# A two-block transformer kernel in fp32: two row norms deferred to the evictions behind them

## The chip, the cores and the metric

The program runs on one core of a Trainium2 chip. The metric is the device time of the whole program in microseconds, from a median of three runs. Engines are named as in the profile: PE is TensorE, DVE is VectorE, ACT is ScalarE, POOL is GpSimd, SP is SyncE, which issues the weight loads. "q" behind a name is the engine's queue, PEld a weight load into the PE array.

## The reference

256 tokens, width 2048, fp32 throughout. Two blocks follow one another; what matters for the change is where the norms stand:

```
# block 1
h = x
h = h + mixer_block(rms_norm(h, norm_mix_w), w_in, ...)      # projections, scan, attention, w_out
u = rms_norm(h, norm_mlp_w)                                  # "norm 1" below
h = h + jnp.square(jax.nn.relu(u @ w_up)) @ w_down
h = rms_norm(h, norm_final_w)
# block 2
h = concatenate([meta_tokens, h])                            # 16 tokens ahead
hn = rmsnorm(h, pre_norm_g)                                  # with the line before: "norm 2"
qa, ka, va, ga, qb, kb, vb, gb = split(hn @ w_in_2)
y = concatenate([axial attention(qa, ka, va) * silu(ga), differential attention(qb, kb, vb) * silu(gb)]) @ w_out_2
out = (h + rmsnorm(y, post_norm_g))[16:]
```

A norm multiplies each row (token) by r = 1/sqrt(mean(row^2) + eps) and each column by a weight. Since r is one number for each token, (r * row) @ W = r * (row @ W), and relu(r * z)^2 = r^2 * relu(z)^2.

## The kernel before

Every product is made from fp32 values split in two: hi is the value rounded to the fp32r format, lo the rest, and three products hi*hi, hi*lo, lo*hi are summed. Weights come in chunks of 256 rows by 512 columns (`raw`, 4 slots). For each chunk ACT makes the upper part (`split_hi`, L695), DVE the lower one (`split_lo`, L986), and PE does its matmuls: `chunk_t` (L351), 24 of them, with the result transposed (features on partitions, 256 tokens as columns, 272 with the meta tokens), or `chunk_n` (L363), 12 with 512 columns and rows as rows. Eight chunks make one column group, whose result lies in one of two PSUM sets of two banks each (`set_free` counts evictions). The split of a chunk waits until PE is done with the chunk four before it, so ACT and DVE, which follow the same program order, run one chunk behind PE's end and three ahead of its need.

The order of all work is written out by hand: each engine has its own list, and side work (scan levels, attention steps) is hung between the chunks of a group. In the second block this is `side(pos)`, where pos counts chunks from column group 6 of the second in-projection: unit u of the attention is scored at one position, exponentiated at the next, normalised on DVE two later, turned on PE three later, multiplied with the values four later. 16 units of the differential attention start at position 0, 16 of the axial one at position 28.

The stages in order: first norm, first in-projection (22 groups) with scan and attention, branches, out-projection (4 groups, `chunk_n`, added onto h by DVE at L1190), **norm 1**, MLP in four quarters (4 groups up, `chunk_t`, ACT relu L845, POOL square L1457; 4 groups down, `chunk_n`, added onto h at L1210), **norm 2**, second in-projection (13 groups, j = 0 to 12; the first five are keys and values, evicted by ACT from 272-column banks), last projection (4 groups) and output.

A norm (`norm`, L701 on ACT, L988 on DVE, `turn_normed`, L371, on PE) runs between two groups: ACT squares each group of h and sums the rows (L699), DVE adds the sums, ACT takes the root (L704), DVE the reciprocal, both scale the rows into `normed` (token tile 0 on DVE at L998, tile 1 on ACT at L708), PE transposes 32 tiles (L381) into banks 4 to 7, ACT writes `xhi` with the column weight (L711), DVE `xlo` (L1001), and the next projection starts on them. For norm 2, h is also multiplied by the final norm's weights, squared once more (L1215, L858), and two scales are combined (L1222 to L1231).

In the second in-projection ACT evicts every group (`evac_in2`, L868): groups 0 to 3 (L873, L877), 4 (L879 to L881), queries (L884), queries with their squares for the rope (L888, L889), and for the gates a sigmoid (L738) that DVE multiplies with the same PSUM data (L1261). In group 8, `rope` on POOL (L1466 to L1472) works on `qg`, which the next eviction overwrites.

## Time and profile before

| | |
|---|---|
| median of 3 runs | 2041.23 us (2040.49 to 2042.9) |
| span of the profiled execution | 2039.5 us |
| PE busy | 1968.3 us, 97% |
| DVE busy | 1124.5 us, 55% |
| ACT busy | 900.0 us, 44% |
| POOL busy | 191.6 us, 9% |
| DMA | 345.29 MB, mean 169 GB/s |
| granted PE clock, by 40 slices | 9 tenths or more in all |

The profile is of one execution; its span is what the views below refer to, and it lies 1.0 to 3.4 us below the three times. Times in the timeline are from the span's start. A busy PE row is the duration of one matmul as modelled; the distance between starts is what a matmul costs in a sequence.

### The profile page before, as it was taken

How to read it: one execution, taken by the hardware profiler on the slowest of the kernel's cores; microseconds unless marked ns; L12 is line 12 of the kernel's file. 1: busy time of each engine (PE TensorE's matmuls, PEld its weight loads, DVE VectorE, ACT ScalarE, POOL GpSimd, SP SyncE). 2: the span in 40 equal slices, each digit the busy share in tenths (PEclk: the TensorE clock that was granted, in tenths of full speed). 3: DMA queues.
4: the chain of work that ended last, by engine and by line, in shares of the span. 5: the costliest groups of instructions: out<-in, count | busy, mean ns of one | idle time of the engine just before them, and what ended most of it. 6: DMA issues, size and time to landing. Idle time of an engine off the chain costs nothing.

```text
span 2039.5 us, 34252 instructions
## 1 busy us (share of the span) xinstructions
PE 1968.3 (97%) x13542; PEld 1802.6 (88%) x13542; DVE 1124.5 (55%) x1185; ACT 900.0 (44%) x1165; POOL 191.6 (9%) x110
## 2 busy tenths in 40 slices
PE   5999999999999998999999999999989999998997
PEld 5989999898899987998998899899869998878986
DVE  4456877476545645445444444544455447686554
ACT  5443333356443445443444344344444335535543
POOL 2002433110000100000000000000000000032100
PEclk9999999999999999999999999999999999999999
DMA  7664555555565564666666666666554654333553
GB/s 195 178 190 144 165 162 165 171 175 150 146 207 176 188 213 136 187 189 190 184 187 187 187 187 186 191 180 194 187 186 124 175 157 127 110 106 113 157 189 129
DMA packets 175089, 345.29 MB, mean 169 GB/s; under 512 B 10896, under 2 KB 11024, under 8 KB 174176
## 3 DMA queue, kind: packets, MB, share of 16 engines
q1 hardware_dynamic: 173184, 337.75, 55.7%
q0 software_dynamic: 1776, 5.64, 1.1%
q8 instruction: 103, 1.69, 0.3%
q14 instruction: 26, 0.21, 0.0%
HBM read 341.25 MB, written 2.10 MB: 168 GB/s over the span
## 4 chain that ended last, share of the span: by engine, by line
PE 91%; DVE 5%; ACT 2%; POOL 1%; issue 1%; DMA 1%; DVEq 0%; SPq 0%; ACTq 0%; POOLq 0%
PE ps L351 53%; PE ps L363 31%; DVE wlo L986 1%; PE ps L408 1%; ACT whi L695 1%; DVE obr L1310 1%; PE ps L621 1%; DMA x_nat<-in_x_dram 1%; DVE rs_hg L1100 1%; DVE qsq L1244 0%; DVE xlo L1001 0%; PE ps L591 0%; PE ps L465 0%; PE ps L609 0%; PE ps L455 0%
## 5 line engine op out<-in xcount | busy, mean ns | idle before, releaser
L986 DVE TENSOR_TENSOR wlo<-raw,whi 128x1024 fp32r<-128x1024 f32 x632 | 809.4, 1289 | 788.5 <-ACT whi L695 788.0
L695 ACT ACTIVATE whi<-raw 128x1024 fp32r<-128x1024 f32 x632 | 664.8, 1059 | 993.2 <-PE ps L351 663.7
L351 PE MATMUL ps<-xhi,whi 128*128 128x256 f32 (+1 forms) x3008 | 859.3, 286 | 9.5 <-DVE wlo L986 3.7
L351 PE MATMUL ps<-xlo,whi 128*128 128x256 f32 (+1 forms) x3008 | 847.1, 282 | 0.0
L351 PE MATMUL ps<-xhi,wlo 128*128 128x256 f32 (+1 forms) x3008 | 846.4, 281 | 0.0
L351 PEld LDWEIGHTS ps<-xhi,whi 128*128 128x128 f32 x3008 | 569.1, 189 | 24.6 <-issue 15.7
L351 PEld LDWEIGHTS ps<-xlo,whi 128*128 128x128 f32 x3008 | 568.8, 189 | 1.9 <-issue 1.0
L351 PEld LDWEIGHTS ps<-xhi,wlo 128*128 128x128 f32 x3008 | 568.3, 189 | 0.0
L363 PE MATMUL ps<-whi,xhi 128*128 128x512 f32 x256 | 101.1, 395 | 0.0
L363 PE MATMUL ps<-whi,xlo 128*128 128x512 f32 x256 | 101.1, 395 | 0.0
L363 PE MATMUL ps<-whi,ya_lo 128*128 128x512 f32 x256 | 101.0, 395 | 0.0
L363 PE MATMUL ps<-wlo,yb_hi 128*128 128x512 f32 x256 | 101.0, 395 | 0.0
L363 PE MATMUL ps<-whi,ya_hi 128*128 128x512 f32 x256 | 101.0, 395 | 0.0
L363 PE MATMUL ps<-wlo,ya_hi 128*128 128x512 f32 x256 | 101.0, 395 | 0.0
L363 PE MATMUL ps<-whi,yb_hi 128*128 128x512 f32 x256 | 101.0, 395 | 0.0
L363 PE MATMUL ps<-whi,yb_lo 128*128 128x512 f32 x256 | 101.0, 394 | 0.0
L363 PE MATMUL ps<-wlo,xhi 128*128 128x512 f32 x256 | 100.6, 393 | 0.0
L1457 POOL TENSOR_TENSOR relu<-relu 128x1024 f32<-128x1024 f32 x16 | 32.2, 2013 | 695.8 <-ACT relu L845 695.8
L1396 POOL TENSOR_TENSOR acc<-acc,masked 128x1024 f32<-128x1024 f32 x14 | 40.0, 2858 | 270.6 <-DVE masked L1082 270.6
L363 PEld LDWEIGHTS ps<-wlo,yb_hi 128*128 128x128 f32 x256 | 48.2, 188 | 11.3
L363 PEld LDWEIGHTS ps<-whi,ya_lo 128*128 128x128 f32 x256 | 48.2, 188 | 11.3
L363 PEld LDWEIGHTS ps<-whi,yb_hi 128*128 128x128 f32 x256 | 48.2, 188 | 11.2
...
## 6 DMA issues: line engine op xcount, KB each, us to landing
...
raw<-in_w_up_dram SPq DMA_DIRECT2D x128, 512.0 KB, 3.8
raw<-in_w_down_dram SPq DMA_DIRECT2D x128, 512.0 KB, 4.2
...
```

The lines of the kernel that those rows point to most:

```text
L351: ins = mm(outs[b], w[:, k % SLOTS, j, cols], v[:, kt, 0:n], start=start, stop=last and j == CK - 1 and i == 2, skip_group_check=True)
L363: ins = mm(ps[:, 2 * s + t, :], v[:, kt, toks], w[:, k % SLOTS, j, :], start=first and j == 0 and i == 0, stop=last and j == CK - 1 and i ...
L408: ins = mm(misc[:, i // 4, (i % 4) * P:(i % 4 + 1) * P], kr[:, hd, toks], qp[:, hd, toks], start=True, stop=True)
L621: mm(ps[:, 7, 0:P], v_meta[:, vh, :], pt2[0:META, u % 2, T:T + P], start=False, stop=True).then_inc(u_pv, 1)
L695: f(whi[:, k % SLOTS], raw[:, k % SLOTS], ACT.Copy).then_inc(whi_ready, 1)
L986: tt(wlo[:, k % SLOTS], raw[:, k % SLOTS], whi[:, k % SLOTS], ALU.subtract).then_inc(wlo_ready, 1)
L1100: nc.vector.reciprocal(rs_hg[:, 2 * i:2 * i + 2, :], rs_hg[:, 2 * i:2 * i + 2, :]).then_inc(hg_rs, 1)
L1310: nc.vector.reciprocal(obr[:, 2 * i:2 * i + 2, :], obr[:, 2 * i:2 * i + 2, :]).then_inc(bn_rs, 1)
L1396: tt(acc[:, half, :], acc[:, half, :], masked[:, half, :], ALU.add).then_inc(hg_acc, 1)
L1457: tt(relu2[:], relu[:], relu[:], ALU.mult).then_inc(up_sq, 1)
```

## The change

Norms 1 and 2 no longer stand between two groups. PE transposes the raw rows of h, one column group at a time, eight 128x128 tiles ahead of the third chunk of the next group (`turn_group`); ACT and DVE write the two parts with the column weights alone (`turned_upper`, `turned_lower`), for norm 1 into new buffers `x2hi`, `x2lo`, for norm 2 into `xhi`, `xlo` with the weight `fin_k`, the product of the final norm's and the second block's weights, which one more small load brings. The per-token scale is applied later. For the MLP its square multiplies each down group on eviction (two DVE operations on 128x512 in place of one on 128x1024). For the second in-projection the scale is wanted along the columns, so DVE makes two diagonal matrices, PE multiplies ones by them after group 0, and DVE copies the result to `row_s`; PE waits for that (`r_ready`) ahead of group 1. DVE then evicts all 13 groups with a multiplication by `row_s`. What ACT did at these evictions it does from SBUF (square and scale of the rope queries) or, for the gates, as a sigmoid that reads DVE's copy and writes PSUM, which DVE multiplies as before. The multiplication of h by the final norm's weights moves to POOL. The PE loops of the out-projection and the first MLP quarter are written out.

The diff, cut to its core (`...` marks what is left out):

```diff
+            def turn_group(b, n, freed):
+                pe.wait_ge(set_free[n % 2], freed)
+                if n >= 2:
+                    pe.wait_ge(x_ready, KT * b + 4 * n - 4)
+                for i in range(4):
+                    kt = 4 * n + i
+                    for t in range(NT):
+                        ins = nc.tensor.transpose(turned(n, i)[:, t * P:(t + 1) * P],
+                                                  h[:, t, kt * P:(kt + 1) * P], ident[:])
+                    if i % 2 == 1:
+                        ins.then_inc(n_tr, 1)
...
-            with pe.Fori(0, 2) as i:
-                for s in range(2):
-                    pe.wait_ge(set_free[s], G_IN // 2 + 4 + i)
-                    for k in range(NC):
+            for n in range(4):
+                pe.wait_ge(set_free[n % 2], G_IN // 2 + 4 + n // 2)
+                for k in range(NC):
+                    if n == 0:
                         pe.wait_ge(br_ready, k // 2 + 1)
-                        chunk_n(C_OUT + 2 * NC * i + NC * s, k, CK * k, xhi, xlo, s, k == 0, k == NC - 1)
-            turn_normed(1)
-            def quarter(q):
+                    if n >= 1 and k == 2:
+                        turn_group(1, n - 1, out_free[n - 1])
+                    chunk_n(C_OUT + NC * n, k, CK * k, xhi, xlo, n % 2, k == 0, k == NC - 1)
...
+                        if first and g == 0:
+                            if k == 2:
+                                turn_group(1, 3, out_free[3])
                             pe.wait_ge(x_ready, KT + CK * (k + 1))
-                        chunk_t(c0 + NC * g, k, CK * k, xhi, xlo, blocks(g % 2), T, k == 0, k == NC - 1)
+                        chunk_t(c0 + NC * g, k, CK * k, x2hi, x2lo, blocks(g % 2), T, k == 0, k == NC - 1)
...
+                        if last and g >= 1 and k == 2:
+                            turn_group(2, g - 1, down_free[g - 1])
...
                     if j == 0:
+                        if k == 2:
+                            turn_group(2, 3, down_free[3])
                         pe.wait_ge(x_ready, 2 * KT + CK * (k + 1))
...
+                if j == 0:
+                    pe.wait_ge(r_diag, NT)
+                    for t in range(NT):
+                        ins = mm(ps[:, 4, t * P:(t + 1) * P], ones[:], diag[:, t, :], start=True, stop=True)
+                    ins.then_inc(r_mm, 1)
...
+            def turned_upper(b, n, dst, w):
+                for i in range(4):
+                    kt = 4 * n + i
+                    act.wait_ge(n_tr, KT // 2 * b + kt // 2 + 1)
+                    f(dst[:, kt, 0:T], turned(n, i), ACT.Copy, scale=w[:, kt:kt + 1]).then_inc(n_hi, 1)
...
             for n in range(4):
                 for k in range(NC):
                     split_hi(C_OUT + NC * n, LEAD + k)
-                h_squares(1, n, G_IN // 2 + 4 + n // 2 + 1, n_ss)
-            norm(1, h, mlp_w, 2)
-            def quarter(q, last):
+                    if n >= 1 and k == 0:
+                        h_squares(n - 1, out_free[n - 1], n_ss, junk_out)
+                    if n >= 1 and k == 1:
+                        turned_upper(1, n - 1, x2hi, mlp_w)
...
+                if j == 4:
+                    act.wait_ge(set_free[0], SETS_BEFORE_2 + 3)
+                    f(qsq[:, 0:2, :], qg[:, 0:2, :], ACT.Square).then_inc(nr_ev, 1)
+                    act.wait_ge(nr_ev, 1)
+                    f(qg[:, 0:2, :], qg[:, 0:2, :], ACT.Copy, scale=gvec[:, 2:3]).then_inc(nr_ev, 1)
                 elif j in (7, 8):
                     n = j - 6
-                    act.wait_ge(nr_done, n)
-                    f(qg[:, :, 0:T], pset(n - 1), ACT.Copy, scale=gvec[:, 1:2]).then_inc(nr_ev, 1)
-                    f(qsq[:, :, 0:T], pset(n - 1), ACT.Square).then_inc(nr_ev, 1)
-                else:
-                    g = (j - 9)
+                    act.wait_ge(nr_raw, n)
+                    f(qsq[:, :, 0:T], qg[:, :, 0:T], ACT.Square).then_inc(nr_ev, 1)
+                    act.wait_ge(nr_ev, 2 * n + 1)
+                    f(qg[:, :, 0:T], qg[:, :, 0:T], ACT.Copy, scale=gvec[:, 1:2]).then_inc(nr_ev, 1)
+                elif j >= 9:
+                    g = j - 9
                     dst = gb if g < 2 else ga
-                    sigmoid(dst[:, 4 * (g % 2):4 * (g % 2) + 4, :], g % 2, e_sig)
+                    act.wait_ge(g_raw, g + 1)
+                    f(pset(g % 2), dst[:, 4 * (g % 2):4 * (g % 2) + 4, :], ACT.Sigmoid).then_inc(e_sig, 1)
...
+                    if j == 0:
+                        if k == 0:
+                            h_squares(3, down_free[3], f_sq, junk)
+                        if k == 1:
+                            turned_upper(2, 3, xhi, fin_k)
+                        if k == 2:
+                            scaled_squares(3)
+                        if k == 3:
+                            act.wait_ge(f_un, 1)
+                            f(ss[:, 4:6], ss[:, 4:6], ACT.Sqrt, bias=eps_t[:], scale=1.0 / D).then_inc(f_un, 1)
+                        if k == 4:
+                            row_root(2, 6)
...
+            def turned_lower(b, n, dst, hi, w):
+                for i in range(4):
+                    kt = 4 * n + i
+                    dve.wait_ge(n_hi, KT * b + kt // 2 * 2 + 2)
+                    stt(out=dst[:, kt, 0:T], in0=turned(n, i), scalar=w[:, kt:kt + 1], in1=hi[:, kt, 0:T],
+                        op0=ALU.mult, op1=ALU.subtract).then_inc(x_ready, 1)
...
-                    hv = h[:, :, g * CW:(g + 1) * CW]
-                    tt(hv, hv, ps[:, 2 * (g % 2):2 * (g % 2) + 2, :], ALU.add).then_inc(set_free[g % 2], 1)
-                    if last:
-                        if g == 0:
-                            dve.wait_ge(finw_in, 16)
-                        dve.wait_ge(f_sq, 2 * (g + 1))
-                        tt(hv, hv, spread(fin_w[:, g * CW:(g + 1) * CW], [0, NT], [1, CW]), ALU.mult).then_inc(f_w, 1)
-            with dve.Fori(0, QUARTERS - 1) as q:
-                quarter(q, False)
-            quarter(QUARTERS - 1, True)
-            nc.vector.tensor_reduce(ss[:, 4:6], sq[:, 1], AX.X, ALU.add).then_inc(f_un, 1)
-            dve.wait_ge(n_ss, 24)
-            own(nc.vector.tensor_reduce(ss[:, 6:8], sq[:, 2], AX.X, ALU.add))
-            dve.wait_ge(f_un, 2)
-            own(nc.vector.reciprocal(rstd[:, 4:6], ss[:, 4:6]))
-            own(tt(ss[:, 6:8], ss[:, 6:8], rstd[:, 4:6], ALU.mult))
-            tt(ss[:, 6:8], ss[:, 6:8], rstd[:, 4:6], ALU.mult).then_inc(n_sum, 1)
-            dve.wait_ge(n_sd, 3)
-            own(nc.vector.reciprocal(rstd[:, 12:14], ss[:, 6:8]))
-            tt(rstd[:, 6:8], rstd[:, 12:14], rstd[:, 4:6], ALU.mult).then_inc(n_rs, 1)
-            norm_tail(2, h, pre_w, 6)
+                    for t in range(NT):
+                        hv = h[:, t, g * CW:(g + 1) * CW]
+                        ins = stt(out=hv, in0=ps[:, 2 * (g % 2) + t, :], scalar=rstd[:, 14 + t:15 + t], in1=hv,
+                                  op0=ALU.mult, op1=ALU.add)
+                    ins.then_inc(set_free[g % 2], 1)
...
+            def row_scales(k):
+                if k == 3:
+                    dve.wait_ge(f_sq, 8)
+                    nc.vector.tensor_reduce(ss[:, 4:6], sq[:, 1], AX.X, ALU.add).then_inc(f_un, 1)
+                    dve.wait_ge(n_ss, 24)
+                    own(nc.vector.tensor_reduce(ss[:, 6:8], sq[:, 2], AX.X, ALU.add))
+                if k == 4:
+                    dve.wait_ge(f_un, 2)
+                    own(nc.vector.reciprocal(rstd[:, 4:6], ss[:, 4:6]))
+                    own(tt(ss[:, 6:8], ss[:, 6:8], rstd[:, 4:6], ALU.mult))
+                    tt(ss[:, 6:8], ss[:, 6:8], rstd[:, 4:6], ALU.mult).then_inc(n_sum, 1)
+                if k == 5:
+                    dve.wait_ge(n_sd, 3)
+                    own(nc.vector.reciprocal(rstd[:, 12:14], ss[:, 6:8]))
+                    own(tt(rstd[:, 6:8], rstd[:, 12:14], rstd[:, 4:6], ALU.mult))
+                    for t in range(NT):
+                        ts(diag[:, t, :], ident[:], rstd[:, 6 + t:7 + t], None, ALU.mult).then_inc(r_diag, 1)
+                if k == 6:
+                    dve.wait_ge(r_mm, 1)
+                    own(nc.vector.memset(row_s[:, T:TM], 1.0))
+                    own(nc.vector.tensor_copy(row_s[:, 0:T], ps[:, 4, 0:T]))
+                    dve.sem_inc(r_ready, 1)
...
             def evac_in2(j):
-                if j < 9:
+                dve.wait_ge(pe_done, C_IN2 + NC * (j + 1))
+                if j in (0, 2):
+                    for s in range(2):
+                        dst = (kb if j == 0 else v_t)[:, 2 * s:2 * s + 2, :]
+                        tt(dst, ps[:, 2 * s:2 * s + 2, 0:TM], rows(2, TM), ALU.mult).then_inc(set_free[s], 1)
+                    return
+                if j in (1, 3):
+                    dst = (kb if j == 1 else v_t)[:, 4:8, :]
+                    tt(dst, ps[:, 4:8, 0:TM], rows(4, TM), ALU.mult).then_inc(kvb_free, 1)
+                    return
+                if j == 4:
+                    tt(qg[:, 0:2, :], ps[:, 0:2, 0:TM], rows(2, TM), ALU.mult).then_inc(set_free[0], 1)
+                    tt(v_t[:, 8:10, :], ps[:, 2:4, 0:TM], rows(2, TM), ALU.mult).then_inc(set_free[1], 1)
+                    return
+                if j in (5, 6):
+                    s = (j - 5) % 2
+                    stt(out=qb[:, 4 * s:4 * s + 4, :], in0=pset(s), scalar=DH ** -0.5, in1=rows(4, T), op0=ALU.mult,
+                        op1=ALU.mult).then_inc(set_free[s], 1)
+                    return
+                if j in (7, 8):
+                    dve.wait_ge(nr_done, j - 6)
+                    tt(qg[:, :, 0:T], pset(j - 7), rows(4, T), ALU.mult).then_inc(nr_raw, 1)
                     return
                 g = j - 9
                 s, half = g % 2, slice(4 * (g % 2), 4 * (g % 2) + 4)
+                dst = (gb if g < 2 else ga)[:, half, :]
+                tt(dst, pset(s), rows(4, T), ALU.mult).then_inc(g_raw, 1)
                 dve.wait_ge(e_sig, N_E1 + g + 1)
-                dst = (gb if g < 2 else ga)[:, half, :]
                 stt(out=dst, in0=pset(s), scalar=subg[:] if g < 2 else 1.0, in1=dst, op0=ALU.mult,
                     op1=ALU.mult).then_inc(set_free[s], 1)
...
+            pool.wait_ge(finw_in, 16)
+            for g in range(4):
+                hv = h[:, :, g * CW:(g + 1) * CW]
+                pool.wait_ge(f_sq, 2 * (g + 1))
+                pool.wait_ge(n_tr, KT + 2 * (g + 1))
+                tt(hv, hv, spread(fin_w[:, g * CW:(g + 1) * CW], [0, NT], [1, CW]), ALU.mult).then_inc(f_w, 1)
```

Order of the instructions on DVE from the eviction of the last down group of the MLP into the second in-projection. Names: `wlo` the lower part of a weight chunk, `h` the rows, `ss`, `sq`, `rstd` row sums and scales. Before:

```order
L1210 TENSOR_TENSOR h<-h,ps 128x2x512
L1215 TENSOR_TENSOR h<-h,fin_w 128x2x512
L1222 TENSOR_REDUCE ss<-sq 128x2
L1224 TENSOR_REDUCE ss<-sq 128x2
L1226 RECIPROCAL rstd<-ss 128x2
L1227 TENSOR_TENSOR ss<-ss,rstd 128x2
L1228 TENSOR_TENSOR ss<-ss,rstd 128x2
L1230 RECIPROCAL rstd<-ss 128x2
L1231 TENSOR_TENSOR rstd<-rstd 128x2
L998 TENSOR_SCALAR normed<-h,rstd 128x512 x4
L1001 SCALAR_TENSOR_TENSOR xlo<-ps,pre_w,xhi 128x256 x16
L986 TENSOR_TENSOR wlo<-raw,whi 128x1024 x3
```

With the change:

```order
L1292 SCALAR_TENSOR_TENSOR h<-ps,rstd,h 128x512 x2
L1052 TENSOR_TENSOR wlo<-raw,whi 128x1024 x2
L1059 SCALAR_TENSOR_TENSOR xlo<-ps,fin_k,xhi 128x256 x4
L1052 TENSOR_TENSOR wlo<-raw,whi 128x1024 x2
L1305 TENSOR_REDUCE ss<-sq 128x2
L1307 TENSOR_REDUCE ss<-sq 128x2
L1052 TENSOR_TENSOR wlo<-raw,whi 128x1024
L1310 RECIPROCAL rstd<-ss 128x2
L1311 TENSOR_TENSOR ss<-ss,rstd 128x2
L1312 TENSOR_TENSOR ss<-ss,rstd 128x2
L1052 TENSOR_TENSOR wlo<-raw,whi 128x1024
L1315 RECIPROCAL rstd<-ss 128x2
```

The rescaled rows and the sixteen evictions in one piece are gone; four evictions of transposed rows stand behind two splits, and the small operations of the scale are spread over the chunks of the group.

ACT at the end of group 7, `whi` the upper part of a chunk, `pt` and `p` the attention's weights. Before:

```order
L923 ACTIVATE pt<-ps 128x256 [waits u_pv,u_t]
L924 ACTIVATE pt<-ps 16x128
L912 ACTIVATE p,rsum<-p,nm 128x272 [waits u_nm]
L912 ACTIVATE p,rsum<-p,nm 128x272
L888 ACTIVATE qg<-ps,gvec 128x4x256 [waits nr_done,pe_done]
L889 ACTIVATE qsq<-ps 128x4x256
L695 ACTIVATE whi<-raw 128x1024 [waits pe_done,raw_in0]
L923 ACTIVATE pt<-ps 128x256 [waits u_pv,u_t]
```

With the change:

```order
L733 ACTIVATE whi<-raw 128x1024 [waits pe_done,raw_in3]
L977 ACTIVATE pt<-ps 128x256 [waits u_pv,u_t]
L978 ACTIVATE pt<-ps 16x128
L966 ACTIVATE p,rsum<-p,nm 128x272 [waits u_nm]
L966 ACTIVATE p,rsum<-p,nm 128x272
L940 ACTIVATE qsq<-qg 128x4x256 [waits nr_raw]
L942 ACTIVATE qg<-qg,gvec 128x4x256 [waits nr_ev]
L733 ACTIVATE whi<-raw 128x1024 [waits pe_done,raw_in0]
```

The two evictions from PSUM became two operations on SBUF, in the other order, and wait for DVE's copy (`nr_raw`) where they waited for PE and POOL; the split of the next chunk stands behind them in both.

DVE at the end of group 9, the first gate (`gb`), `p` and `nm` the attention's weights and maxima. Before:

```order
L986 TENSOR_TENSOR wlo<-raw,whi 128x1024
L1291 RECIPROCAL rinv<-rsum 128x1
L1292 TENSOR_SCALAR p<-p,rinv 128x272
L1277 TENSOR_REDUCE nm<-ps 128x1
L1278 TENSOR_SCALAR nm<-nm 128x1
L1261 SCALAR_TENSOR_TENSOR gb<-ps,subg,gb 128x1024
L986 TENSOR_TENSOR wlo<-raw,whi 128x1024
```

With the change:

```order
L1052 TENSOR_TENSOR wlo<-raw,whi 128x1024
L1408 RECIPROCAL rinv<-rsum 128x1
L1409 TENSOR_SCALAR p<-p,rinv 128x272
L1394 TENSOR_REDUCE nm<-ps 128x1
L1395 TENSOR_SCALAR nm<-nm 128x1
L1376 TENSOR_TENSOR gb<-ps,row_s 128x1024
L1378 SCALAR_TENSOR_TENSOR gb<-ps,subg,gb 128x1024
L1052 TENSOR_TENSOR wlo<-raw,whi 128x1024
```

One operation is added ahead of the multiplication, and ACT's sigmoid waits for it.

## Rows read from the trace of the kernel before

**Rows 1.** the page's chain of work that ended last, shares of the span by engine

```profile
PE 91%; DVE 5%; ACT 2%; POOL 1%; issue 1%; DMA 1%; DVEq 0%; SPq 0%; ACTq 0%; POOLq 0%
```

**Rows 2.** waits of PE: who was waited for, us in total, times, longest

```profile
PE ps L381 <- ACT normed L708: 36.4, 3, 18.8
PE ps L351 <- ACT qsq L880: 2.3, 1, 2.3
```

**Rows 3.** timeline around norm 1: start us, us, engine, line, op, out<-in, [idle before]

```profile
788.46 0.40 PE L363 MATMUL ps<-whi,xlo 128*128 128x512 f32 x1
791.18 1.21 DVE L1190 TENSOR_TENSOR h<-h,ps 128x1024 f32 x1
802.61 0.37 PE L351 MATMUL ps<-xhi,whi 128*128 128x256 f32 x1
```

**Rows 4.** timeline around norm 2, the same columns

```profile
1522.01 0.40 PE L363 MATMUL ps<-whi,yb_lo 128*128 128x512 f32 x1
1522.51 1.06 ACT L695 ACTIVATE whi<-raw 128x1024 fp32r<-128x1024 f32 x1 [1.73 <-PE ps L363]
1524.74 1.21 DVE L1210 TENSOR_TENSOR h<-h,ps 128x1024 f32<-128x1024 f32 x1
1538.55 0.37 PE L351 MATMUL ps<-xhi,whi 128*128 128x272 f32 x1
```

**Rows 5.** windows, the stretch of norm 2: us, busy (x) by engine, PEclk, DMA

```profile
1522.00:1539.00 17.00, 7.00 (x37) 6.27 (x36) 10.48 (x26) 11.66 (x29) 0.00 (x0) 0.70 0.24 75
```

**Rows 6.** timeline of PE, transposes in column group 5, three from one row to the next

```profile
1671.71 0.27 PE L553 MATMUL ps<-ident,v_t 128*128 128x128 f32 x1
1672.04 0.27 PE L553 MATMUL ps<-ident,v_t 128*128 128x128 f32 x1
```

**Rows 7.** chain of waits: start us, us, what; and timeline, a DVE copy

```profile
153.31 3.57 PE ps L408 x32
1674.20 0.42 DVE L1237 COPY v_nat<-ps 128x256 f32<-128x256 f32 x1
```

**Rows 8.** timeline at the end of column group 4

```profile
1660.39 1.23 DVE L986 TENSOR_TENSOR wlo<-raw,whi 128x1024 fp32r<-128x1024 f32 x1 [1.77 <-ACT whi L695]
1660.86 0.61 ACT L880 ACTIVATE qsq<-ps 128x544 f32<-128x544 f32 x1
```

**Rows 9.** timeline at the end of column group 7

```profile
1768.56 0.72 DVE L1275 TENSOR_REDUCE nm<-p 128x2 f32<-128x544 f32 x1
1769.17 1.06 ACT L695 ACTIVATE whi<-raw 128x1024 fp32r<-128x1024 f32 x1 [0.32 <-PE ps L351]
```

**Rows 10.** timeline at the end of column group 8, and PE in group 9

```profile
1803.73 1.12 ACT L888 ACTIVATE qg<-ps,gvec 128x1024 f32<-128x1024 f32 x1 [5.11 <-POOL qa L1472]
1806.74 1.23 DVE L986 TENSOR_TENSOR wlo<-raw,whi 128x1024 fp32r<-128x1024 f32 x1 [5.38 <-ACT whi L695]
1830.11 1.28 PE L601 MATMUL ps<-ka,qa 128*128 128x272 f32 x2 [5.08 <-ACT p L915]
```

**Rows 11.** timeline, POOL and DVE together in column group 8

```profile
1793.59 3.39 POOL L1466 TENSOR_TENSOR qg<-qg,cos_t 128x1024 f32<-128x1024 f32 x1
1794.64 1.21 DVE L1252 TENSOR_TENSOR qrot<-ps,sin_t 128x1024 f32<-128x1024 f32 x1
1795.85 2.22 DVE L986 TENSOR_TENSOR wlo<-raw,whi 128x1024 fp32r<-128x1024 f32 x1
```

**Rows 12.** timeline, DVE at the ends of column groups 9 and 10

```profile
1845.20 1.28 DVE L1261 SCALAR_TENSOR_TENSOR gb<-ps,subg,gb 128x1024 f32<-128x1024 f32 x1
1884.31 1.28 DVE L1261 SCALAR_TENSOR_TENSOR gb<-ps,subg,gb 128x1024 f32<-128x1024 f32 x1 [1.12 <-ACT gb L738]
```

**Rows 13.** chain of waits, start of the last projection; timeline after column group 12

```profile
1938.83 89.25 PE ps L363 x384
1941.16 1.22 DVE L1261 SCALAR_TENSOR_TENSOR ga<-ps,ga 128x1024 f32<-128x1024 f32 x1
1947.17 2.35 DVE L986 TENSOR_TENSOR wlo<-raw,whi 128x1024 fp32r<-128x1024 f32 x2
```

174 lines of the change are left out of this document (103 added, 71 removed).

## Prediction

> **What bounds the kernel now.** I read the page's chain of waits first: TensorE (PE) holds 91% of the chain that ended last [rows 1]. So only what PE executes or waits for counts, and the view for that is PE's own waits. There the largest entry by far is 36.4 us in three waits, each for the normalised rows in front of the transposes [rows 2]: one at the start of the kernel, which the change leaves alone, one ahead of the MLP (norm 1) and one ahead of the second in-projection (norm 2), which it takes apart. The timeline then gives the whole hole, not only the wait. Matmuls of a row-form chunk start 2.79 / 12 = 0.23 us apart (1.06 busy + 1.73 idle on ScalarE (ACT) is one chunk [rows 4]). Norm 1: the last matmul starts at 788.46, so PE could go on at 788.69, and the next projection starts at 802.61: **13.9 us** [rows 3]. Norm 2: 1522.01 + 0.23 to 1538.55: **16.3 us** [rows 4]. In this hole the granted clock averages 0.70 [rows 5]: PE had fallen to its lower level (1.2 GHz), so the transposes in it were also dearer than in the middle of work.
>
> **The change, part by part.**
>
> *The holes go.* 13.9 + 16.3 = -30.2 us, with all that lies in them: squares, roots, rescaled rows, 64 transposes. The root, the reciprocals and the scale products are still made, but on ACT and VectorE (DVE) inside groups.
>
> *The transposes come back.* Eight groups of eight, each ahead of the third chunk of the next column group. Where PE does transposes between two chunks at full clock, three take 0.33 us, 0.11 each [rows 6]: 64 x 0.11 = +7.0 us. I expect no wait in front of them. A group is released by the eviction of its columns, about 3.7 us after the group's end (1524.74 + 1.21 against 1522.24 [rows 4]), and PE reaches the third chunk after 2 x 2.79 = 5.6 us. Their evictions on ACT and DVE lie in engines that are idle 1.7 of 2.79 us per chunk [rows 4]. So norm 1 is bounded between 13.9 - 3.5 = 10.4 gained and less by any wait; I take 10.4.
>
> *A stall that the norm hid: start of in-projection 2.* Its first group writes all four banks of both PSUM sets, so it waits for the eviction of the last down group. Nothing covers that now. That eviction ended at 1524.74 + 1.21 = 1525.95, and PE could start at 1522.24 [rows 4]; two 128x512 operations in place of one 128x1024 add little: **+3.8 us** (3.7 to 4.0). Ahead of the MLP there is no such stall, as its first group takes one set, which was evicted a group earlier.
>
> *The scale row.* After the first in-projection group PE multiplies ones by the diagonal matrices, DVE copies 128x256 out of PSUM, and only then may the second group start. Sixteen 128x128 products, 32 records, take 3.57 us, so two take 0.45 [rows 7]; the copy takes 0.42 [rows 7]; with a memset and four hand-overs between engines I take **+1.4 us**. Bounds: 0.9 (the two alone) and 2.1 (if DVE is still in a 1.2 us split). The diagonals themselves are due at the sixth chunk and are wanted after the eighth, some 5 us later, so they should not be late.
>
> *Evictions move from ACT to DVE.* DVE does one behind its last split of a group, where ACT did it beside that split. The price is paid only where somebody waits at once:
> - group 4 to 5: PE waited 2.3 us for ACT's second eviction [rows 2], which ended at 1661.47. DVE's split ends near 1661.55, and a 128x544 copy at the rate of 128x1024 in 1.21 is 0.7: 1662.25. **+0.8** (0.7 to 0.9) [rows 4, 8].
> - group 5 to 6: the first attention scores want the queries one chunk later; the same shift of one DVE operation, partly hidden behind the chunk: **+0.5** (0 to 0.9).
> - group 7 to 8: DVE finishes its softmax step at 1768.56 + 0.7 = 1769.25 [rows 9], then copies (1.2), then ACT squares and scales (1.0 + 1.1): ACT is free at 1772.6, where it began its next split at 1769.17 [rows 9]. That is 3.4 late. The PE steps behind it were due one chunk later, so most of it is covered; I take **+0.7** (0 to 3.4).
> - group 8 to 9: before, ACT waited 5.11 us for POOL, then ran two evictions from 1803.73 [rows 10]. Now DVE copies first (1.2), ACT's two follow. The split behind them on DVE started at 1806.74 after 5.38 us of waiting for ACT [rows 10], and DVE then has reciprocals without a pause up to PE's wait of 5.08 us, which ends at 1830.11 [rows 10]. So the extra copy is on the path in full: **+1.4** (1.2 to 2.3).
> - groups 9 and 10: the gate now goes DVE, ACT, DVE. DVE's last step came at 1845.20 and 1884.31, the latter after 1.12 us of waiting for the sigmoid [rows 12]; it comes 2.3 and 1.2 later. PE wants DVE's unit work a chunk later: **+0.7 and +0.8** (0 to 2.3 each).
> - group 12 to the last projection: the gate's chain (DVE, POOL, ACT, DVE) ends one copy plus one sigmoid later, 2.3 us. The fifth chunk's split then ends at 1947.17 + 1.2 + 2.3 = 1950.7; PE, which starts at 1938.83, wants it at 1938.83 + 4 x 2.79 = 1950.0: **+0.7** (0 to 2.3) [rows 13].
> - groups 0 to 3, 6 and 11: 0. The next user of those banks comes a whole group later; there is only DVE time, of which more than 1 us per chunk is free.
>
> *Moved to GpSimd (POOL):* the multiplication of h by the final norm's weights, four times. At 128x1024 with two inputs POOL takes up to 3.39 us beside DVE [rows 11]. It is due before the squares three chunks later, so it costs 0 by itself. What it does to DVE is the place to weigh a rule. The row first: with POOL at work from 1793.59 to 1796.98, a DVE operation with one input in PSUM took its usual 1.21, but a split, with both inputs in SBUF, took 2.22 in place of 1.23 [rows 11]. So each multiplication may hold up one split by up to 3.4 us. A split is made about three chunks, 8.4 us, ahead of its use, and the evictions read PSUM: cost 0, bound 0 to 3.4 per piece. The Trainium skill (SBUF — State Buffer, section "SBUF: two separate sides") says that the pair of ports which the two engines share is an exclusive lock, held for the whole instruction, so that the loser waits in full. The 2.22 agrees with a wait for POOL's end (1796.98) and not with shared bandwidth; by that rule every one of the four would cost DVE a wait of POOL's whole rest, which is the bound just given and the third rival below.
>
> *The other edits* (one more small load at the start, one product on DVE, the per-token scale squared into the down evictions, the loops written out) lie on engines that PE does not wait for: 0.
>
> **The sum.** -30.2 + 7.0 + 3.8 + 1.4 + 0.8 + 0.5 + 0.7 + 1.4 + 0.7 + 0.8 + 0.7 = **-12.4 us**. The profiled span is 2039.5; the median of the three times is 2041.23, 1.7 above it, and I put the same difference on both sides: 2041.2 - 12.4 = **2028.8 us**, 0.6% faster. With every unknown at its low end the costs are 7.0 + 3.7 + 0.9 + 0.7 + 0 + 0 + 1.2 + 0 + 0 + 0 = 13.5 and the time 2024.5; with every one at its high end 7.0 + 4.0 + 2.1 + 0.9 + 0.9 + 3.4 + 2.3 + 2.3 + 2.3 + 2.3 = 27.5 and 2038.5.
>
> **Rivals.**
> 1. *The evictions give back more.* The softmax steps run as a chain over PE, DVE and ACT with about a chunk of slack. If group ends 7 to 12 cost near their high ends, 3.4 + 2.3 + 2.3 + 2.3 + 2.3 = 12.6 in place of 4.3, the result is 2037. For it: this stretch already has waits of 5 us [rows 10], and a longer one brings the lower clock with it. Against: DVE has free time in most chunks. Full form unlikely; half of it gives 2033.
> 2. *Slower: ACT blocked at every group end.* The wait for DVE's copy stands on ACT in front of the next split and of the copy that PE's next value product wants. If none of the 3.4 us of group 7 is covered, and the same holds at the eight group ends 5 to 12, that is 27.2, with 3.8 + 1.4 + 0.8 + 7.0 = 40.2 against 30.2: **2051 us**. It decides as soon as the delay passes the one chunk (2.8 us and the side work) by which PE lags ACT. Against it: only at groups 7 and 8 do two ACT operations follow the copy.
> 3. *The port.* Each multiplication on POOL delays a split by 3.4 us and PE with it: 4 x 3.4 = 13.6, giving 2042.4, no change. It decides where a split has under 3.4 us to spare; here it has 8.4.
> 4. *The change does not unhook the norms.* PE waits for the eviction in front of each of its eight transposing groups. At 1 us each that is 8 and the time 2037; it needs the eviction over 5.6 us after the group's end, and it came after 3.7.
>
> **How the numbers follow.** A measurement of this kernel can tell about 0.2%, 4 us, from no change. Forecast (2024.5 to 2031.5): 0.64. Rival 1, mostly 2031.5 to 2037: 0.22, of which 0.02 ends above 2037. Rival 4: 0.03, its half above 2037. Rival 3: 0.04. Rival 2: 0.05. Something that no row shows, either way: 0.02. Faster by over 0.2% (below 2037.1) is then 0.64 + 0.20 + 0.015 + 0.01 = 0.87, slower 0.05 + 0.01 = 0.06, the rest 0.07. The range, 2024 to 2037, leaves out rivals 2 and 3 and the tails, under 2 in 10.
>
> **What would show it.** No wait of PE for the normalised rows but the first, of about 18 us. Transposes of h in eights with starts 0.11 us apart and no idle time ahead of them. A wait of PE of about 3.8 us at the start of in-projection 2 for DVE's eviction, and about 1 us ahead of its second group for the scale row. Group 4 to 5 waiting 3.1 us in place of 2.3. From group 7 on, waits of PE that sum to some 4 us more than before. It is wrong if the transposes wait, if the gap ahead of the MLP stays over 1 us, or if the stretch from the start of in-projection 2 to the end is over 12 us longer than before, counted without the holes.

## The result, and the profile after

The changed kernel takes 2012.6 us (median of 4, 2009.1 to 2017.4) against 2042.0 (median of 4, 2040.5 to 2042.9) for the one before: 0.9857 of the time (95% interval 0.9839 to 0.9875), 29 us less. I had predicted 2028.8, range 2024 to 2037. The direction was right, the time is 16 us below the forecast and 11 below the range. The profiled execution has a span of 2015.6 us, 23.9 under the one of before. Of the experiments below, one execution of e10 (2034 us, at a granted clock of 0.94 where its others have 0.99) is left out of its median.

First the entries that answer to the forecast's waits. PE's waits after the change (us in total, times, longest), beside [rows 2]:

```profile
PE ps L408 <- ACT normed L757: 18.3, 1, 18.3
PE ps L630 <- ACT p L969: 6.5, 1, 6.5
PE ps L638 <- DVE p L1409: 5.3, 2, 4.7
PE ps L365 <- issue: 4.7, 3, 3.9
...
PE ps L365 <- DVE qg L1361: 3.1, 1, 3.1
...
PE ps L365 <- DVEq L1323: 0.7, 1, 0.7
```

Of the three waits for normalised rows the first is left. The 3.9 "for issue" is the start of the second in-projection, group 4 to 5 waits 3.1, the scale row 0.7. The transposes, in the timeline of PE inside the out-projection, against [rows 6]:

```profile
725.78 0.40 PE L377 MATMUL ps<-whi,xlo 128*128 128x512 f32 x1
726.02 1.03 PE L393 MATMUL ps<-ident,h 128*128 128x128 f32 x8
726.81 0.47 PE L377 MATMUL ps<-whi,xhi 128*128 128x512 f32 x1
```

Eight of them, no idle time ahead, 0.79 us from the first to the next product's start. And the start of the second in-projection, which answers to [rows 4]:

```profile
1501.90 1.40 DVE L1292 SCALAR_TENSOR_TENSOR h<-ps,rstd,h 128x512 f32<-128x512 f32 x2
1503.51 0.36 PE L365 MATMUL ps<-xhi,whi 128*128 128x272 f32 x1 [3.94 <-issue]
...
1504.21 0.39 PE L365 MATMUL ps<-xhi,wlo 128*128 128x272 f32 x1
1504.39 0.43 PE L365 MATMUL ps<-xhi,whi 128*128 128x272 f32 x1
```

and in the windows view (us, PE busy, PEld, DVE, ACT, POOL, granted clock, DMA share, GB/s) just behind it:

```profile
1504.40:1507.40 3.00, 3.00 (x15) 3.00 (x15) 0.00 (x0) 0.00 (x0) 0.00 (x0) 0.50 0.25 94
```

The wait is the one forecast. What follows it was not: from 1504.39 on the matmuls start 0.23 us apart in place of 0.12. That is the lower level of PE's clock (granted 0.50 in the row above), which the hole of norm 2 before also had in part [rows 5]. Over the 27.9 us from the restart the granted clock averages 0.94.

**Where the 23.9 us went.** The chain of waits gives one piece for each unbroken run of PE (start, us, what, count of matmuls). Before:

```profile
577.50 122.42 PE ps L351 x1032
699.92 88.96 PE ps L363 x384
788.96 1.06 ACT whi L695
...
802.86 90.36 PE ps L351 x768
893.21 89.23 PE ps L363 x384
983.01 90.62 PE ps L351 x768
...
1522.51 1.06 ACT whi L695
...
1538.80 120.42 PE ps L351 x960
```

After:

```profile
580.07 118.32 PE ps L365 x1032
698.38 27.80 PE ps L377 x120
...
789.98 5.47 PE ps L365 x48
...
877.94 87.89 PE ps L377 x384
965.83 87.07 PE ps L365 x768
...
1143.97 88.38 PE ps L365 x749
1232.35 89.60 PE ps L377 x384
...
1499.67 1.06 ACT whi L733
...
1892.13 22.80 PE ps L365 x192
```

(The last projection of before starts at 1938.83 [rows 13], the one of after where the last piece shown ends, at 1914.93.)

| stage, from the starts of these pieces | before | after | difference |
|---|---|---|---|
| start to the branches' piece | 577.5 | 580.1 | +2.6 |
| branches (with the end of the first in-projection) | 122.4 | 118.3 | -4.1 |
| out-projection | 89.0 | 91.6 | +2.6 |
| norm 1 | 13.9 | 0 | -13.9 |
| MLP | 719.7 | 709.7 | -10.0 |
| norm 2 / stall in its place | 16.3 | 3.8 | -12.5 |
| second in-projection | 400.0 | 411.4 | +11.4 |
| last projection and output | 100.7 | 100.7 | 0 |

The surprise stands in rows that the change doesn't touch: the same 1032 matmuls of the branches in 118.3 us instead of 122.4. In the MLP, 32 transposes were added, and it is 10 us shorter. 768 up matmuls take 87.07 in place of 90.62, 384 down 87.89 in place of 89.23. The last projection tells the same: one of its chunks takes 2.75 in place of 2.79. The clock is not it; the two rows are the windows view of an up stretch, before and after (columns as above):

```profile
803.00:893.20 90.20, 90.20 (x768) 90.20 (x768) 43.40 (x40) 39.14 (x40) 6.03 (x3) 1.00 0.62 175
```

```profile
965.90:1052.90 87.00, 87.00 (x769) 87.00 (x768) 43.67 (x37) 39.24 (x38) 6.07 (x3) 1.00 0.64 194
```

Nor is it a wait: PE is busy throughout, and the distance between starts is shorter, 87.07 / 768 = 0.1134 us against 0.1180 (0.1177 in the groups behind the first). I call this PE's step. The third quarter (1143.97, 1232.35) runs at 88.38 / 749 = 0.1180 again, in the same code as the second. So there are two things to find: what sets the step, and why the third quarter differs.

### The profile page after: what moved, and what is told of

The parts are those of the page before. It is cut to its first block, busy times and chain, and to the rows that moved or that the text cites. A ratio compares the mean times of both kernels' runs of the same rounds, so it can differ in the third digit from the quotient of the medians.

```text
span 2015.6 us, 34070 instructions
## 1 busy us (share of the span) xinstructions
PE 1954.3 (97%) x13546; PEld 1794.1 (89%) x13546; DVE 1143.8 (57%) x1211; ACT 889.0 (44%) x1148; POOL 204.3 (10%) x115
## 4 chain that ended last, share of the span: by engine, by line
PE 91%; DVE 5%; ACT 2%; issue 1%; DMA 1%; POOLq 0%; POOL 0%; DVEq 0%; SPq 0%; ACTq 0%
PE ps L365 54%; PE ps L377 30%; DVE wlo L1052 2%; PE ps L435 1%; ACT whi L733 1%; DVE obr L1427 1%; DMA x_nat<-in_x_dram 1%; DVE rs_hg L1171 1%; PE ps L650 0%; PE ps L492 0%; PE ps L620 0%; PE ps L482 0%; PE ps L393 0%; PE ps L638 0%; PE ps L474 0%
## 5 line engine op out<-in xcount | busy, mean ns | idle before, releaser
L365 PE MATMUL ps<-xhi,whi 128*128 128x256 f32 (+1 forms) x1984 | 577.1, 291 | 14.3 <-issue 3.9
L365 PE MATMUL ps<-xhi,wlo 128*128 128x256 f32 (+1 forms) x1984 | 564.4, 284 | 0.0
L365 PE MATMUL ps<-xlo,whi 128*128 128x256 f32 (+1 forms) x1984 | 564.2, 284 | 0.0
L365 PEld LDWEIGHTS ps<-xhi,whi 128*128 128x128 f32 x1984 | 380.8, 192 | 29.0 <-issue 20.1
L365 PE MATMUL ps<-x2lo,whi 128*128 128x256 f32 x1024 | 284.1, 277 | 0.5 <-issue 0.5
L365 PE MATMUL ps<-x2hi,whi 128*128 128x256 f32 x1024 | 284.3, 278 | 0.2 <-issue 0.2
L365 PE MATMUL ps<-x2hi,wlo 128*128 128x256 f32 x1024 | 284.2, 277 | 0.0
L365 PEld LDWEIGHTS ps<-x2lo,whi 128*128 128x128 f32 x1024 | 193.4, 189 | 0.1
L365 PEld LDWEIGHTS ps<-x2hi,whi 128*128 128x128 f32 x1024 | 192.3, 188 | 0.8 <-DVE wlo L1052 0.7
L365 PEld LDWEIGHTS ps<-x2hi,wlo 128*128 128x128 f32 x1024 | 192.3, 188 | 0.6 <-issue 0.6
```

Of the source, the lines that this page charges most:

```text
L365: ins = mm(outs[b], w[:, k % SLOTS, j, cols], v[:, kt, 0:n], start=start, stop=last and j == CK - 1 and i == 2, skip_group_check=True)
```

## Experiments

From here on a group's length is the distance between two starts of ACT's first split behind a group, 8 chunks of PE apart. Four theories: **A**, the step depends on the addresses of the tiles; **B**, on PE's code being written out; **C**, on chance; and, against all, on the deferral itself. A has a concrete hook: the change allocates `fin_k`, 64 bytes per partition, among the persistent tiles, and every tile behind it moves by 64 bytes. Worked out from the kernel's own allocations, ya_hi lies 75392 bytes behind whi before and 75456 after. I give such distances modulo 256: 128 before, 192 after. xhi and xlo don't move, and with their rows of 1088 bytes the distance takes 0, 64, 128 and 192 in turn.

### First four: addresses or code

e1, the kernel before with the 64 bytes alone:

```diff
         pre_w = sb("pre_w", [P, KT])
+        spare = sb("spare", [P, 16])
```

> The kernel before with one unused tile of 64 bytes per partition allocated behind pre_w, nothing else; every later tile moves by 64 bytes, as it does in the changed kernel. Theory A (addresses: PE's step depends on where the moving or stationary tiles lie against whi and wlo): branches at 21.8 us per group in place of 22.8 (4 x -1.0), down groups 22.0 in place of 22.3 (16 x -0.34), last projection -1.4; up groups stay at 22.6, since xhi and xlo do not move: -11 us, 2031. Theory B (the PE code written out, or where it lies in memory): no change, 2041. Theory C (chance from one execution to the next): pace may differ between the runs by 5 us or more, without regard to the edit.

e2, the changed kernel with one more such tile behind `fin_k`:

> The changed kernel with one more unused tile of 64 bytes behind fin_k, so that the later tiles lie at multiples of 128 bytes again, as before. Theory A: the pace of before comes back in branches, MLP and last projection: about +4 (branches), +10 to +13 (up, at 22.6 to 22.8 a group), +5 (down), +1.4: some 20 us, 2030 to 2036. Theory B: no change, 2009 to 2017. Theory C: spread as after has it, 2009 to 2017.

e3, the kernel before, with the weights moved by 64 bytes and all tiles behind them by 128, which gives the distance of e1, 192, at other addresses:

```diff
+        spare = sb("spare", [P, 16])
         whi = sb("whi", [P, SLOTS, CK, CW], F32R)
         wlo = sb("wlo", [P, SLOTS, CK, CW], F32R)
+        spare_2 = sb("spare_2", [P, 16])
```

> The kernel before with 64 unused bytes ahead of whi and 64 behind wlo: only whi and wlo stand at an odd multiple of 64, all other tiles keep their place against 128 bytes. Theory A in its relative form (the distance between weights and x counts): as e1, -11 us, 2031. Theory A in its absolute form (where the branch and MLP inputs lie counts): no gain, 2041 or slower if whi and wlo themselves are better at multiples of 128. Theory B and C: 2041.

e4, the kernel before with PE's code written out:

```diff
-            with pe.Fori(0, 2) as i:
-                for s in range(2):
...
+            for n in range(4):
...
-            with pe.Fori(0, QUARTERS - 1) as q:
+            quarter(0)
+            with pe.Fori(1, QUARTERS - 1) as q:
```

> The kernel before with PE's out-projection and first MLP quarter written out as in the changed kernel, tiles where they were. Theory A: no change, 2041. Theory B: the pace of the changed kernel from the first quarter on, 21.8 a group up and 22.0 down: about -14 us, 2027.

| | median, us | ratio to before | 95% |
|---|---|---|---|
| e1 | 2034.6 | 0.996 | 0.9946 to 0.9974 |
| e2 | 2030.3 | 0.9934 | 0.9917 to 0.995 |
| e3 | 2030.1 | 0.9935 | 0.9918 to 0.9951 |
| e4 | 2043.9 | 1.0008 | 0.9998 to 1.0018 |

B is out: e4's interval takes in 1, and its groups have the lengths of before. e1 gained 8 of the 11 us that A had forecast; e2 and e3 came out as A had them. An unused tile of 64 bytes makes the kernel before 8 us faster, and another one makes the changed kernel 18 us slower (2012.6 to 2030.3). The pieces of the chain of e1 for the branches, the first up and the first down groups:

```profile
576.42 118.31 PE ps L352 x1032
...
797.69 90.37 PE ps L352 x768
888.06 87.90 PE ps L364 x384
```

The branches and the down groups have the changed kernel's lengths to 0.01 us; up, from the unmoved xhi, has that of before. e3 shows the same at the same distance, with both moved (down 87.90 too):

```profile
578.99 118.28 PE ps L353 x1032
```

In e2 the distance is 0, and here the two forms part:

```profile
578.80 123.42 PE ps L366 x1032
...
973.89 92.15 PE ps L366 x768
1066.05 87.06 PE ps L378 x384
```

Up is at its slowest (0.1200 a matmul), down, with the weights as moving operand, at its fastest (0.2267). The inputs of the branches and of the down groups lie at the same addresses in e2 and e3, 128 bytes behind those of before, and the branches take 123.42 and 118.28; the weights lie at the same addresses in e1 and before, and they take 118.31 and 122.42. So it is the distance between the weights and the other operand that counts, not where either lies. The Trainium skill (SBUF — State Buffer, section "Who interferes with whom") gives PE two read ports that are independent, one for the moving operand and one for the weights. That neither bears on the other is hard to square with these runs, which differ only in where tiles lie; what couples them a profile does not show.

### The fourth distance, and the buffers alone

e5 is e1 with `spare` of 192 bytes, distance 64:

> The kernel before with an unused tile of 192 bytes behind pre_w, so that the distance from whi to ya, yb and the later tiles is 64 modulo 256, the one of the four that no run has shown (128 before: 22.8 us per branch group and 22.3 down; 192: 21.8 and 22.0; 0 in the changed kernel shifted by 64: 23.0 and 21.8). If an odd multiple of 64 is what counts: 21.8 and 22.0, 2034 as with 64 bytes. If the distance modulo 128 does not say it all: another pair of values, 2030 to 2046.

2045.6 us, 1.0015 of before (1.0006 to 1.0025). A had forecast 2034 if an odd multiple of 64 is what counts. Branch groups take 22.61, down 22.40:

```profile
576.91 121.73 PE ps L352 x1032
...
891.98 89.59 PE ps L364 x384
```

So an odd multiple of 64 is not enough. e8 takes the changed kernel's buffers without its deferral: e1, with norm 1 writing x2hi and x2lo, which the up groups read:

```diff
+        x2hi = at("x2hi", 48, [P, KT, T], F32R)
+        x2lo = at("x2lo", 64, [P, KT, T], F32R)
-        normed = at("normed", 56, [P, NT, D])
+        normed = at("normed", 88, [P, NT, D])
...
-                        chunk_t(c0 + NC * g, k, CK * k, xhi, xlo, blocks(g % 2), T, k == 0, k == NC - 1)
+                        chunk_t(c0 + NC * g, k, CK * k, x2hi, x2lo, blocks(g % 2), T, k == 0, k == NC - 1)
```

> The kernel before with the 64 bytes and with the MLP's input written to buffers of their own, x2hi and x2lo, as the changed kernel has them (row pitch 1024, 192 modulo 256), but with both norms where they were. Theory A: up groups 21.8 in place of 22.6, 16 x -0.83 = -13 against the kernel with the 64 bytes alone, 2021. What is then left to the changed kernel (2012.6) is the deferral itself: -9, by its parts holes -30, transposes +7, waits and dearer evictions +14. If the deferral brings the pace: no gain from the buffers, 2034.

2030.2 us, 0.9932 (0.9905 to 0.996), between the two forecasts (2021 and 2034), and from 2018.6 to 2035.6 over six executions. The profiled one (span 2027.5) shows a reason:

```profile
797.95 90.46 PE ps L354 x768
888.42 89.60 PE ps L366 x384
...
1159.44 87.33 PE ps L354 x768
1246.77 87.89 PE ps L366 x384
...
```

One address, one loop, and two steps: the first two quarters at 0.1178 and 0.2333, the others at 0.1137 (0.1134 in the fourth) and 0.2289. This is the changed kernel's third quarter again, the other way round. At distance 192 PE has two steps, and the slower ones are those of distance 64. The last run of the next series, e12, shows that 64 has both too.

### Is it the jump back?

e6 is the changed kernel with all four quarters written out on PE (no loop in the MLP):

> The changed kernel with all four MLP quarters written out on PE. If the slower third quarter of the profiled run (22.6 and 22.4 a group in place of 21.8 and 22.0, behind the jump back of PE's loop) comes of the jump, it is gone in every run: 2007 to 2010 with a spread under 3 us. If it is chance without regard to the jump, the times still spread over 8 us, 2009 to 2017.

2008.8 us (2007.7 to 2010.3), 0.9834 (0.9815 to 0.9853): in its profile every quarter is fast, and the 8 us between the changed kernel's times are gone. Here the third one:

```profile
1139.87 87.07 PE ps L365 x768
```

### Using it: rows of 256

e7 is the changed kernel with xhi and xlo read with rows of 1024 bytes wherever only 256 columns are wanted, moved so that the distance is 192. The 16 meta columns lie behind them and are copied to their places during the MLP.

```diff
+        spare = sb("spare", [P, 48])
+        xhi_f = sb("xhi", [P, KT * TM], F32R)
+        xlo_f = sb("xlo", [P, KT * TM], F32R)
+        spare_2 = sb("spare_2", [P, 16])
...
+        xhi, xlo = [as_rows(v[:], TM) for v in (xhi_f, xlo_f)]
+        x1hi, x1lo = [as_rows(v[:, 0:KT * T], T) for v in (xhi_f, xlo_f)]
+        mhi, mlo = [as_rows(v[:, KT * T:KT * TM], META) for v in (xhi_f, xlo_f)]
...
-                        chunk_t(c0, k, CK * k, xhi, xlo, blocks(s), T, k == 0, k == NC - 1)
+                        chunk_t(c0, k, CK * k, x1hi, x1lo, blocks(s), T, k == 0, k == NC - 1)
```

> The changed kernel with xhi and xlo read at a row pitch of 1024 bytes, at 192 modulo 256 from whi, in the first in-projection and the out-projection (the meta columns kept behind them and copied to their places in the MLP); with the pitch of 1088 the distance takes all four values in turn. Theory A: chunk_t groups of the first in-projection at 21.8 in place of 22.6, 17 or 18 of them -0.8 each, chunk_n groups 22.0 in place of 22.2: 15 to 17 us faster than the changed kernel, 1993 to 2000. If the distance is not the cause: no gain, 2009 to 2017.

2004.6 us, 0.9813 (0.9795 to 0.9831): 8 faster than the changed kernel, not 15 to 17. Groups 2 to 13 of the first in-projection came as expected, the chunk_t ones at 21.76 where they were 22.59. But group 21 takes 22.61, and the branches are in the slower step, where the changed kernel was in the faster one, and so are the up groups of two quarters (not their down groups), the last of them behind no jump:

```profile
567.04 121.75 PE ps L374 x1032
...
1309.70 90.45 PE ps L374 x768
```

The step of the branches is not chance: at distance 192 they are fast in all seven profiles in which the first in-projection reads rows of 1088 bytes (the changed kernel, e1, e3, e6, e8, e11, e15) and slow in all five with rows of 256 columns (e7, e9, e10, e13, e14). What comes before a stage has a part in it.

### The stall, a third use, and distance 64 in the changed kernel

e9 joins e6 and e7.

> The two edits that helped, together: x rows of 256 in the first in-projection and the out-projection, and the MLP of PE written out. If slow quarters at distance 192 come only of the jump back: every MLP group 21.8 and 22.0, 2008.8 - 12 = 1997. If a stage can also enter its slow step (22.6 or 22.4 a group) without a jump, as the branches of the run with x rows of 256 did, it stays near 2000 to 2004.

1998.3 us (1996.8 to 2000.6), 0.9787 (0.9771 to 0.9804). The MLP is fast in full, the branches stay slow.

e10 adds weights with a pitch of 2112 bytes per 512 columns in the second in-projection:

```diff
+            far = isinstance(c0, int) and C_IN2 <= c0 + k < C_OUT2
+            return w_rows[0][far][:, k % SLOTS], w_rows[1][far][:, k % SLOTS]
```

> As the one before, and in the second in-projection whi and wlo at a pitch of 2112 bytes per 512 columns, so that with x rows of 1088 bytes the distance stays 192 for every row. Theory A: groups 1 to 4 at 23.1 in place of 24.1 (a step of 0.120 in place of 0.1255), the eight groups of 256 columns some 0.8 less each where PE does not wait: -8 to -11 against the one before. Rival: the copy and split at two blocks of 512, or waits in the attention, take it back: -4 to 0.

1997.2 (1997.2 to 1998.7 in three executions), 0.9781 (0.9762 to 0.9801): the same as e9, where 8 to 11 less was forecast, a miss. The groups of 272 columns go from 24.08 to 23.81 only, and 1 us is lost in the last group of the MLP, where the layout turns over. It looks like the slower step at this width too; no run shows the faster one there.

e11 is e6 with the first two chunks of the second in-projection done by halves, so that the stall is covered:

```diff
+                for s in range(2):
+                    if s == 1:
+                        pe.wait_ge(set_free[1], SETS_BEFORE_2)
+                    for k in range(2):
...
+                            for b in (2 * s, 2 * s + 1):
```

> The changed kernel with the MLP written out, and with the first two chunks of the second in-projection done first for the two banks that are free (set 0), then for the two that wait for the last eviction. If the stall at its start is that eviction alone: 3.8 us of wait gone, group 0 at 27 in place of 30.7 to 31.6, 2005. If the lower granted clock behind the stall was the part I had not counted (1.8 us): another 1 to 2, 2003.

2003.1 us (2000.0 to 2005.1), 0.9804 (0.9788 to 0.982), 5.7 below e6. Group 0 takes 26.03 in place of 31.59. PE's wait is down to 0.8, and the granted clock of the stretch is 1.00 (windows view, columns as above):

```profile
PE ps L397 <- DVE h L1311: 0.8, 1, 0.8
```

```profile
1493.00:1520.00 27.00, 25.98 (x206) 25.53 (x204) 15.38 (x25) 13.33 (x23) 2.40 (x1) 1.00 0.55 163
```

In the changed kernel it was this:

```profile
1503.50:1531.40 27.90, 27.18 (x204) 26.99 (x204) 13.90 (x22) 12.87 (x22) 2.39 (x1) 0.94 0.47 133
```

So the stall of 3.8 us cost 5.6 in the changed kernel's profile, the wait and 1.8 of lower clock behind it: group 0 takes 30.67, a group without either 24.13 and its transposes 0.88. e6's profile had lost 6.6 there, and e11 gets 5.6 of them back. The Trainium skill (TensorE: Matmul & The Clock Gate, section "What's actually happening") has the idle engine fall to half rate; the trace agrees.

e12 is the changed kernel with 128 unused bytes behind `fin_k`:

> The changed kernel with 128 unused bytes behind fin_k: distance 64 in place of 192. If 64 has the same two steps as 192 and which one comes is set at the entry of a stage: quarters of either kind, 2010 to 2028. If 64 is always the slower one (22.6 up, 22.4 down): the branches +3.4, 12 up groups +0.85, 12 down groups +0.4 and 4 of the last projection: 2028 in every run, spread under 3.

2033.5 us, 0.996 (0.9945 to 0.9976); 2029.7 to 2035.5 in the four executions that this is the median of, and one of 7919 us, which I can't explain. That is above both forecasts (2010 to 2028, or 2028). Branches, up and down are in the slower step, but the up groups of the third quarter, behind a jump, in the faster one (85.05 / 749 = 0.1135):

```profile
577.17 121.73 PE ps L366 x1032
...
1154.98 85.05 PE ps L366 x749
```

### What puts PE into one of its two steps?

Transposes inside a group were my last candidate: in e7 and e9 the out-projection's groups go from 22.46 (the first) to 22.87, of which 0.88 is transposes, and in e9 PE's pieces on either side of the first eight are 28.00 / 120 = 0.2333 and 21.99 / 96 = 0.2291. e13 joins e9 and e11 (best so far), e14 adds eight spare transposes of the identity in group 21 to it, e15 adds eight in the second up group of every quarter to e8:

```diff
+                    if g == G_IN - 1 and k == 2:
+                        for i in range(8):
+                            nc.tensor.transpose(ps[:, 4, i % 4 * P:(i % 4 + 1) * P], ident[:], ident[:])
```

> The changed kernel with x rows of 256, the MLP written out and the first two chunks of the second in-projection by halves. If the three add up: 1998.3 - 5.7 = 1992.6. If the half chunks' gain hangs on the state before it: 1995 to 1998.

> As the one before, with eight spare transposes of the identity ahead of the third chunk of group 21, the last of the first in-projection. If transposes inside a group put PE into its faster step at distance 192: the rest of group 21 and the four branch groups at 21.8 in place of 22.6, -0.6 - 3.4 + 0.9 = -3.1. If they do not: +0.9.

> The kernel before with the 64 bytes and x2hi, x2lo (2018.6 to 2035.6, its first two quarters at 22.6 and 22.4), with eight spare transposes ahead of the third chunk of the second up group of every quarter. If transposes put PE into its faster step: all four quarters at 21.8 and 22.0 from there on, 4 x 0.9 us of transposes more: 2018 to 2023, spread under 5. If the step is chance: as before, 2018 to 2036 and 3.6 later.

e13: 1994.3 us (1992.3 to 1994.7), 0.9758 (0.9742 to 0.9774), 4.0 below e9 in place of 5.7, between the two forecasts; its group 0 takes 26.00 where e9 had 30.71, so 4.7 was there to be gained. e14: 1996.7 (1992.7 to 1997.8), 0.977 (0.9752 to 0.9788); group 21 went from 22.61 to 23.49, which is the transposes, and the branches stayed at 22.61: no effect on the step. e15: 2033.5 (2032.0 to 2035.6), 0.9957 (0.994 to 0.9974), within the range forecast for chance. In its profile the second and the third quarter come to the transposes alike, with pieces of 27.49 and 27.48 us for 240 matmuls (0.1145, with the first rows behind the jump). Behind them the second stays in the faster step, 59.86 / 528 = 0.1134, and the third falls into the slower one, 62.19 / 528 = 0.1178:

```profile
980.61 27.49 PE ps L354 x240
...
1008.97 59.86 PE ps L354 x528
...
1157.13 27.48 PE ps L354 x240
1185.48 62.19 PE ps L354 x528
```

The first quarter is slow on both sides of its transposes, the fourth fast on both. So the step can flip at transposes, to fast in e9's out-projection and to slow here, and the theory that they make it fast falls. What decides is **open**. Lengths of a group of 8 chunks, us, without transposes:

| distance, modulo 256 | chunk_t, 256 columns | chunk_n | seen in |
|---|---|---|---|
| 0 | 23.04 | 21.76 | e2 |
| 64 | 22.61 or 21.76 | 22.40 | e5, e12 |
| 128 | 22.78 | 22.31 | before, e4 |
| 192 | 22.61 or 21.76 | 22.40 or 21.97 | after, e1, e3, e6 to e11, e13 to e15 |
| all four in turn | 22.59 | 22.24 | xhi, xlo as they were |

## Why the prediction was wrong

**The step that failed** is one that the sum held without saying so: "-30.2 + 7.0 + ...", with everything else at the durations of the trace before. It took for granted that a matmul which the change does not touch keeps its step. The row that I used for it (2.79 / 12 = 0.23 [rows 4]) was one of several possible values, set by where tiles lie, and the diff moved nearly all of them: it allocates one small tile in the middle, and gives norm 1 buffers of its own with another row pitch. The forecast put "the other edits", among them "one more small load at the start", at 0, as lying on engines that PE does not wait for; it was this load's tile that moved the rest, and it changed what PE itself takes. In its place the runs show this, by the groups of the profiled execution: branches -4.1; up groups 12 x -0.83, the third quarter's four unchanged; down groups 12 x -0.34 and 4 x +0.09; last projection 4 x -0.34. Together -19 us. With the third quarter fast as well it is 4 x 0.85 + 4 x 0.43 = 5.1 more: the changed kernel's times are 2009.1, 2009.7, 2015.4 and 2017.4, and e6 has 2008.8. e1 and e3 show the branches' and down groups' part without any deferral, e8 that of the up groups in its last two quarters.

**What is left of the deferral** at equal steps, term by term, against the forecast:

| term | forecast | measured |
|---|---|---|
| holes of norms 1 and 2 | -30.2 | -13.9 - 16.3 = -30.2 |
| 64 transposes | +7.0 | +0.88 to 0.89 a group of 8: +7.1 |
| start of in-projection 2 | +3.8 | +3.8, and 1.8 of lower clock behind it |
| scale row | +1.4 | +1.4 (group 1 of in-projection 2, 25.55 against 24.1) |
| groups 5 to 11 of in-projection 2 | +4.9 | +5.4 to +7.1 |
| last projection, first group | +0.7 | +1.3 |
| sum | -12.4 | -9.4 to -7.7 |

The mechanism of the deferral was right, and in this profile its sum is 3 to 5 us too hopeful. How much of that is the evictions is not settled: against e1, groups 5 to 11 are longer by 5.4 in the changed kernel's profile, by 3.9 in e6's and by 2.5 in e11's. The 1.8 is the term I left out: [rows 5] had shown that a hole brings the lower clock, and I charged that only to the hole that went. The groups 5 to 11 have a spread of their own: group 5 takes 30.4 in the kernel before and 31.9 in e1 with the same code, and from 31.2 (e11) to 33.9 in the kernels with the deferral. Single pieces: group 4 to 5 waits 3.1 (forecast 2.3 + 0.8), the first queries are waited for 0.9, the wait for ACT behind group 8 is 6.5 where it was 5.1, and the one for DVE after it 4.7 where it was 5.2. With -7.7 to -9.4 alone the time would have been 2032 to 2034 and in my range.

Two runs bear this out without a table of terms. e12 has the deferral, e5 has not, and both are at distance 64, with branches at 22.61, down groups at 22.40 and up groups at 22.61 and 22.59, save e12's third quarter (21.76, worth 3.3). Their medians are 2033.5 and 2045.6, their profiled spans 2027.9 and 2042.2: the deferral itself is worth 8.8 us by the medians, 11.0 by the profiles. So the direction was no luck; that the time moved by 29 us was not the forecast's mechanism.

One of the signs that I had named for being wrong came true. From the start of in-projection 2 to the end, the stall included and the holes not, it is 516.2 us after against 501.0 before, 15.2 longer, where 12 was the limit. Over the forecast are the lower clock (1.8), groups 5 to 11 (7.1 in place of 4.9) and the last projection's first group (1.3 in place of 0.7). One reading was off by 0.07: DVE's split at the end of group 4 ends at 1660.39 + 1.23 = 1661.62 [rows 8], not near 1661.55, which changes no term.

The 2.6 us at the start are no cost of the change: group 1 of the first in-projection takes 25.67 in the kernel before's profile, 27.17 in e4 and e6, 28.36 in the changed kernel and 25.67 again in e12, with the same code.

**The rivals.** Rival 1 in small part: the evictions of groups 5 to 11 cost 5.4 to 7.1 in this profile instead of 4.9, where it had 12.6 for the ends of groups 7 to 12 alone. Rivals 2 and 4 did not come. Of rival 3 the first half came and the second did not. Each of POOL's four multiplications of h (mean 2.4 us) holds up one split on DVE, which takes 3.31 to 3.35 us in place of 1.23 and ends 1.1 after POOL does:

```profile
1437.53 2.40 POOL L1584 TENSOR_TENSOR h<-h,fin_w 128x1024 f32<-128x1024 f32 x1 [24.35 <-PE ps L393]
1437.66 3.35 DVE L1052 TENSOR_TENSOR wlo<-raw,whi 128x1024 fp32r<-128x1024 f32 x1 [1.52 <-ACT whi L733]
```

But no chunk of PE is late for it: the down groups with transposes are 22.86 = 21.97 + 0.89. Transposes wait for nothing. None of them, and no tail that I gave a chance, had the time below 2024; "something that no row shows, either way" had 0.02.
